# Three sums of squares a tile, from VectorE to ScalarE, in an expert retrieval that streams its rows by indirect DMA

## The reference

```
y   = gelu(y);  y = y * sigmoid(y @ w_glu + b_glu)        # 512 wide
mix = concat(rmsnorm(attn, g_attn), rmsnorm(y, g_ssm));   x = x + mix @ w_out
xn  = rmsnorm(x, g_ffn)
q   = xn @ w_query; s = q . sub_keys; per head (8): top 16 of each half,
      the 16 best of their sums -> idx, gate = softmax(best)     # 128 experts a token
out = x + sum_k gate_k * gelu(u_table[idx_k] . xn) * v_table[idx_k]
y   = rmsnorm(out, g_final)
rmsnorm(x, g) = x * (mean(x*x) + 1e-5) ** -0.5 * g
```

## Time and profile before

| | |
|---|---|
| median of three runs | 3325.18 us |
| profiled execution, its own time | 3328.39 us |
| its span, first to last instruction | 3326.6 us |
| PE matmul busy | 2289.7 us (69%) |
| VectorE (DVE) busy | 2177.2 us (65%) |
| GpSimd (POOL) busy | 1330.7 us (40%) |
| ScalarE (ACT) busy | 936.3 us (28%) |
| share of 16 DMA engines by the gathers' queue | 84.0% |
| bytes | 1216.94 MB, mean 366 GB/s |

### The profile page before, as it was taken

How to read it: one execution, slowest core, us unless ns; L and a number is a source line. 1 busy time by engine, 2 the same in 40 slices (tenths; PEclk the granted TensorE clock), 3 DMA queues, 4 the chain that set the end, 5 groups by cost and what they waited for, 6 DMA issues and landing times.

```text
span 3326.6 us, 31891 instructions
## 1 busy us (share of the span) xinstructions
PE 2289.7 (69%) x9269; PEld 938.1 (28%) x9269; DVE 2177.2 (65%) x5175; ACT 936.3 (28%) x3200; POOL 1330.7 (40%) x1272
## 2 busy tenths in 40 slices
PE   8997675766685668566855685568566855685576
PEld 4555451331151115111511151115111511151121
DVE  4544539788667756775677567756776676568654
ACT  2222114323332222222322232322232223222222
POOL 1241014434443444344434443444444444444442
PEclk9999787886896779687978797889688978797799
DMA  5223269999999999999999999999999999999998
GB/s 192 84 72 88 75 270 358 386 386 402 419 419 415 417 400 417 416 417 402 419 416 417 400 419 415 416 398 419 413 413 418 419 402 420 397 408 411 420 420 338
DMA packets 188351, 1216.94 MB, mean 366 GB/s; under 512 B 27272, under 2 KB 30712, under 8 KB 47456
## 3 DMA queue, kind: packets, MB, share of 16 engines
q0 software_dynamic: 157600, 1143.05, 84.0%
q1 hardware_dynamic: 30576, 71.86, 6.0%
HBM read 1199.15 MB, written 15.55 MB: 365 GB/s over the span
## 4 chain that ended last, share of the span: by engine, by line
DMA 33%; PE 22%; DVE 17%; issue 7%; ACT 5%; POOL 3%; another core or an unknown queue 0%; DVEq 0%; POOLq 0%; PEldq 0%; ACTq 0%; SPq 0%
DMA uv_ring<-in_uv_table,idx 33%; PE ACC L1998 14%; DVE uv_ring L1823 9%; PE TQ L1937 5%; POOL uv_ring L1465 3%; ACT dg L1598 2%; PE OP L1918 1%; ACT dot L1591 1%; PE TQ L1959 1%; ACT dot L1578 1%; DVE pos L1668 1%; DVE idx_f L1744 1%; DVE pos L1665 1%; DVE S L1743 1%; DVE best L1667 0%
## 5 line engine op out<-in xcount | busy, mean ns | idle before, releaser
L1998 PE MATMUL ACC<-uv_ring,dg 128*64 128x512 f32 x4352 | 1440.2, 772 | 932.5 <-ACT dg L1598 932.3
L1465 POOL DMA_INDIRECT uv_ring<-in_uv_table,idx x1088 | 1234.1, 1134 | 1611.2 <-PE ACC L1998 1375.1
L1823 DVE CUSTOM_DVE_ANT_0 uv_ring<-uv_ring,xn 128x1024 f32<-128x1024 f32 x1088 | 1326.5, 1226 | 738.2 <-DMA uv_ring<-in_uv_table,idx 675.5
L1998 PEld LDWEIGHTS ACC<-uv_ring,dg 128*64 128x64 f32 x4352 | 339.4, 164 | 1925.4 <-ACT dg L1598 1405.6
L1578 ACT ACTIVATE dot<-dot 128x2 f32<-128x2 f32 x544 | 110.5, 203 | 1853.6 <-DVE dot L1823 1838.8
L1598 ACT ACTIVATE dg<-stack,dot 128x64 f32<-128x64 f32 x1088 | 326.4, 340 | 17.8
L1591 ACT ACTIVATE dot<-gate,dot 128x1 f32<-128x1 f32 x1088 | 261.1, 287 | 18.9
L1937 PEld LDWEIGHTS TQ<-glu_and_queries,wq 128*128 128x128 f32 x2048 | 237.0, 194 | 63.9 <-issue 63.9
L1937 PE MATMUL TQ<-glu_and_queries,wq 128*128 128x128 f32 x2048 | 250.5, 281 | 0.0
L527 PE MATMUL PJ<-w_in,xT 128*128 128x512 f32 (+1 forms) x384 | 142.7, 528 | 3.2 <-DVE pj L407 3.2
L527 PEld LDWEIGHTS PJ<-w_in,xT 128*128 128x128 f32 x384 | 72.2, 191 | 68.1 <-issue 65.2
(11 more groups left out here) (336 smaller groups left out, 1640.2 us busy)
## 6 DMA issues: line engine op xcount, KB each, us to landing
uv_ring<-in_uv_table,idx POOLq DMA_INDIRECT x1088
glu_and_queries<-in_w_glu SPq DMA_DIRECT2D x9, 1024.0 KB
wq<-in_w_query SPq DMA_DIRECT2D x8, 1024.0 KB, 19.5
w_in<-in_w_in SPq DMA_DIRECT2D x8, 640.0 KB, 11.0
xt<-in_x SPq DMA_DIRECT2D x9, 512.0 KB, 4.7
xr<-scratch_x SPq DMA_DIRECT2D x9, 512.0 KB
xc<-in_x_columns SPq DMA_DIRECT2D x8, 512.0 KB, 3.8
xk<-in_x SPq DMA_DIRECT2D x8, 512.0 KB, 3.5
```

Of the source, the lines that this page charges most:

```text
L1465: pool.indirect_dma_start(out=ring[:, s_ % RING, :], out_offset=None, in_=a["uv_table"], in_offset=bass.IndirectOffsetOnAxis(ap=idx[:, s_: ...
L1823: V.tensor_tensor_reduce(row, row, xn[:, g, :], 1.0, 0.0, ALU.mult, ALU.add, dot[:, s_:s_ + 1]).then_inc(dots, 1)
L1998: ins = nc.tensor.matmul(ACC[GT * g:GT * (g + 1), b, :], dg[:, n % DG, :], ring[:, n % RING, D + 512 * b:D + 512 * b + 512], start=False, ...
```

## The change

The three sums of squares are taken by ScalarE as `Square` with `accum_out`, in the output tiles that VectorE used. The square of y stands at step (1, 4), that of x at (2, 7), that of the output at the end of ScalarE's turn, behind `begin(t + 1)` (the gelu, weights and diagonals of slots 0 and 1). VectorE's means move to (1, 6), (2, 9) and, as `mean_out`, to slot LEAD + 1 = 4 of the next tile; for the samples it follows `sum_out` directly. The later steps move on: POOL's roots to (1, 6) and (2, 9) and gather 12; VectorE's scaling of y to (1, 12) and of x to (2, 14); PE's turning of y from (1, 11) to (1, 14); VectorE's multiplication of turned y from (1, 13) to (1, 15); the scaling of the output from slot 6 to slot 8. `xr_done` is now marked by the second addition to x.

```diff
-        OUT_AT = LEAD + 3
+        OUT_AT = LEAD + 5
@@ POOL
-                        if turn != "first" and s_ == RING + LEAD:
+                        if turn != "first" and s_ == RING + LEAD + 1:
                             root("o", t - 1, ms_o, rs_o)
...
-                                if (h, j) == (1, 3):
+                                if (h, j) == (1, 6):
                                     root("y", t_, ms_y, rs_y)
-                                if (h, j) == (2, 6):
+                                if (h, j) == (2, 9):
                                     root("x", t_, ms_x, rs_x)
@@ ScalarE
+                    elif at == (1, 4):
+                        k["y_gated"].of(act, t)
+                        k["ss_y_done"].mark(A(z[:], y[:], ACT.Square, accum_out=ss_y))
+                    elif at == (2, 7):
+                        k["xr_done"].of(act, t)
+                        k["ss_x_done"].mark(A(xn_next[:], xr[:], ACT.Square, accum_out=ss_x))
...
                     if turn != "samples":
                         begin(t + 1)
+                    n = NS_ROWS if turn == "samples" else P
+                    k["acc_taken"].of(act, t)
+                    k["ss_o_done"].mark(A(squares[0:n, :], xo[0:n, :], ACT.Square, accum_out=ss_o[0:n]))
@@ VectorE
-                        dch_(V.tensor_tensor(y[:], y[:], z[:], ALU.mult))
-                        dch_(V.tensor_tensor_reduce(z[:], y[:], y[:], 1.0, 0.0, ALU.mult, ALU.add, ss_y))
+                        k["y_gated"].mark(V.tensor_tensor(y[:], y[:], z[:], ALU.mult))
+                    elif at == (1, 6):
+                        k["ss_y_done"].of(dve, t)
                         k["ms_y_done"].mark(V.tensor_scalar(ms_y, ss_y, 1.0 / SW, EPS, ALU.mult, ALU.add))
-                    elif at == (1, 9):
+                    elif at == (1, 12):
...
-                    elif at == (1, 13):
+                    elif at == (1, 15):
                         k["yn_turned"].of(dve, t)
...
-                        dch_(V.tensor_tensor(xr[:, 512:D], OP[:, 1, :], xr[:, 512:D], ALU.add))
-                        k["xr_done"].mark(V.tensor_tensor_reduce(xn_next[:], xr[:], xr[:], 1.0, 0.0, ALU.mult, ALU.add, ss_x))
-                        k["xr_done"].of(dve, t)
+                        k["xr_done"].mark(V.tensor_tensor(xr[:, 512:D], OP[:, 1, :], xr[:, 512:D], ALU.add))
+                    elif at == (2, 9):
+                        k["ss_x_done"].of(dve, t)
                         k["ms_x_done"].mark(V.tensor_scalar(ms_x, ss_x, 1.0 / D, EPS, ALU.mult, ALU.add))
-                    elif at == (2, 12):
+                    elif at == (2, 14):
...
-                    k["acc_taken"].of(dve, t)
-                    k["ss_o_done"].mark(V.tensor_tensor_reduce(squares[0:n, :], xo[0:n, :], xo[0:n, :], 1.0, 0.0,
-                                                               ALU.mult, ALU.add, ss_o[0:n]))
+
+                def mean_out(t, n):
+
                     k["ss_o_done"].of(dve, t)
                     k["ms_o_done"].mark(V.tensor_scalar(ms_o[0:n], ss_o[0:n], 1.0 / D, EPS, ALU.mult, ALU.add))
...
                         product(t, s_)
+                        if s_ == LEAD + 1 and turn != "first":
+                            mean_out(t - 1, P)
...
                         sum_out(t, NS_ROWS, t * NSLOT + slots_of(turn))
+                        mean_out(t, NS_ROWS)
                         norm_out(t, NS_ROWS)
@@ PE
-                    elif at == (1, 11):
+                    elif at == (1, 14):
                         k["yn_done"].of(pe, t)
```

More of the change, by code:

```diff
@@ L1367, in retrieve_experts @@
             "idx_ready idx_rest best_shifted ex_done gate_ready gate_rest xn_spread_a xn_spread_b xn_taken_a xn_taken_b acc_begun acc_taken "
-            "ss_o_done out_ready out_stored ms_y_done ms_x_done ms_o_done rs_y_done rs_x_done rs_o_done").split()}
+            "ss_o_done out_ready out_stored y_gated ss_y_done ss_x_done ms_y_done ms_x_done ms_o_done rs_y_done rs_x_done rs_o_done").split()}
         first = {n: c.sem(f"first_{n}") for n in "q qT s S topped nmax ex idx gate".split()}
@@ L1623, in begin @@
                         diagonal(t, s_)
-                for n in ("y_gelu yT_done gate_y xnT_done qT_a qT_b qT_c qT_d S_a S_b ex_done "
+                for n in ("ss_y_done ss_x_done ss_o_done y_gelu yT_done gate_y xnT_done qT_a qT_b qT_c qT_d S_a S_b ex_done "
                           "xn_taken_a xn_taken_b").split():
@@ L1862, in _ @@
                 for n in ("zb_done yn_done ynT_done xr_done xn_done topped_a topped_b idx_ready idx_rest best_shifted gate_ready gate_rest "
-                          "acc_taken ss_o_done out_ready ms_y_done ms_x_done ms_o_done").split():
+                          "acc_taken y_gated out_ready ms_y_done ms_x_done ms_o_done").split():
                     k[n].prime(dve)
```

## The result

Over 20 runs of each kernel on one chip the changed kernel takes 3330.5 us and the one before 3320.2 us, medians. The ratio is 1.0032, 95% interval 1.0021 to 1.0043: 10.5 us slower, 7 to 14. (Two of the changed kernel's 20 runs, 3538 and 7658 us, are slow ones and don't count in the ratio; without them its median is 3330.1 us.) The forecast was 3331.5 us against a median of 3325.2, so 6.3 us slower; that was the right side, at 0.6 of the size. The prediction took anything under 17 us as not to be told from no change; 20 runs of each tell 10.5 us from none. The profiled execution has a span of 3332.3 us.

A forecast was written before the change was run, and what follows sets the result against it. The prediction took the DMA engines to bound the kernel. Its terms, 0.4 (start and end) + 2.4 (tile 0) + 3.5 (x) + 0 (boundary) = 6.3 us, on 3325.2 gave 3331.5 us, spanning 3325 to 3343; 8-in-10 range 3310 to 3350.

The forecast's parts named there:

- What bounds the kernel: From tile 1 on the DMA engines set the pace; 128 gathers take 320 us of a tile's 331.
- The output norm at the boundary: At the tile boundary VectorE's wait for the root shrinks from 3.2 to about 1 us; gain 0, at best 3.5.
- The wait at slot 15: VectorE waits 5.5 us for turned y; the batch of 16 and 17 starts 3.0 us late, hidden by the lead.
- nothing covers it: Upper bound at gather 30 if no lead hides the delay: 3.0 us a tile, 21 us lost.
- the term of 0.5 us a tile: At gather 30, 1.7 us late, part is covered: 0.5 us lost in each of seven tiles, +3.5 us.
- Given on to x: The output projection comes 3 us late too, so VectorE's wait for it grows by up to 3 us a tile.
- Tile 0: VectorE is nearly always busy there; the turning makes it 4.5 us late, less the squares of y and x: +2.4 us.
- Before the first gather and at the end: Nothing covers ScalarE's squares there; handoffs cost 0.15 us for y, 0.1 for x, 0.15 for the last output: +0.4 us.
- the chain at its word: Rival: boundary work taken off VectorE shortens every tile, 3.4 x 7 = 24 us, giving 3301 us; chance 0.12.
- The table rival: Rival: Square needs another table than Gelu, so each square adds two loads: 3341 us, 3350 by the page; chance 0.05.
- That PE makes the delay up: Rival: PE catches up, 4 us gained at slot 30 and 3.5 at 1190, giving 3320 us; chance 0.05.
- The rival in which the wait starves the ring: Rival: slot 15's 3.0 us a tile aren't hidden, 21 us, plus 4.5 in tile 0, giving 3351 us; chance 0.20.

The follow-up runs named there:

- run 7: The kernel before with only the output's part of the change: its square on ScalarE, later mean, root and norm; 3326.7 us, ratio 0.9992.
- run 2: The kernel before, all squares on VectorE, with y turned at (1, 14) and multiplied at (1, 15); 3342.5 us, ratio 1.0078.
- run 8: The kernel before with only x's part of the change: its square on ScalarE, later mean, root and scaling; 3328.7 us, ratio 0.9994.
- Run 3: The changed kernel with VectorE's multiplication of turned y at (2, 0) instead of (1, 15), turning left at (1, 14); 3320.4 us, ratio 1.0003.
- Runs 1: The early turning: the changed kernel with PE turning y at (1, 12) instead of (1, 14); 3317.1 us, ratio 0.9995.
- Run 5: The changed kernel, late turning kept, with VectorE's addition to x, ScalarE's square and the mean two slots later; 3336.3 us, ratio 1.0024.
- run 9: The changed kernel with y turned at (1, 12) and the steps of x two slots later; 3321.1 us, ratio 0.9986.
- run 4: The changed kernel with y turned at (1, 12), except in tile 0's turn, which keeps (1, 14); 3316.5 us, ratio 0.9993.

## Why the prediction was right, and where its size was off

- **What bounds the kernel:** right. Every kernel here follows how full the DMA engines are: from the four with the least loss in the stretch (-0.1 to 2.2 us, ratios 0.9986 to 1.0002) to the three with the most (19.8 to 24.5 us, 1.0032 to 1.0078). VectorE's busy time does not order them: the changed kernel has 32 us less of it and is slower. The sign that I had named, a DMA share of 1.00 or more in tiles 1 to 7, held (1.00 or 1.01 in each); it is too coarse, for the rate fell in five of the seven tiles, in tile 2 from 413 to 408 GB/s.
- **The output norm at the boundary:** the wait fell as forecast (0.3 us in the mean), and the gap from gather 7 to gather 8 stayed: 6.0 us in tile 2 after, 6.3 before. The gain was taken as 0, at best 3.5. The two profiles have 3.9 us at the boundary and run 7 gives 2.7, with an interval that reaches no change. That the 3.9 us come from the output's part is not shown: in the same 28 us windows run 2, which has the old output norm, reaches 389.9 GB/s and run 8, which has it too, 386.3, as much as run 7's 386.3. So a gain of 0 isn't refuted.
- **The wait at slot 15:** right in place and size. 5.5 us were reckoned; tiles 1 to 7 have 5.1 to 6.2. So is what follows in tile 2, where the batch of 16 and 17 and gather 24 come 2.8 us late against the 3.0 reckoned. Over the seven tiles gather 24 is 2.8 to 6.3 us late, 4.2 in the mean.
- **The step that was mis-sized** is "*Gathers 24 and 25 are 3 us late. The lead hereabouts is far above 6.3 ...: hidden*", and with it the term of 0.5 us a tile, 3.5 in all. The profiles show 14.8 us, 2.1 a tile, which is nearer to the 3.0 of "nothing covers it" than to my 0.5. I read one lead, at slot 16, and took the next from slot 30. Between them it falls: in tile 2 before, the gathers of slots 24, 26 and 28 have 13.1, 9.1 and 8.4 us, the last two already within 3 us of the least. After, gather 26 was issued at 1226.65 and used at 1234.50, 7.9 us, and the engines had run dry around it. Gather 30, on which I put the whole loss, is over 2.4 us late in only three tiles of seven, and in tile 2 its lead rose from 6.3 to 9.1 us. I had written that I am wrong if a second hole opens around slots 24 to 32. The two short windows of tile 2 show such holes, so by that sign this step was wrong. Run 3 shows that the cover isn't nothing either: of 3.1 us of wait most is covered, of 5.7 it is not. Runs 1 and 2, and 5 against 9, show that this wait is the cause.
- **Given on to x:** the projection was late and VectorE's wait for it grew, by 28 us over tiles 1 to 7, 4.0 a tile, where I had said up to 3. I had read the 17.7 us before as a wait that these tiles have already; 8.9 of it stand ahead of the first gather. And it was not through this second wait that the loss came, as I had it (gather 30). Run 5 took it away and kept the loss.
- **Tile 0:** 2.4 us were reckoned, from a delay of 4.5. The wait is 3.4 us in the kernel after, and run 4 sees no cost of it, but can't tell 2.4 from 0.
- **Before the first gather and at the end:** too small to see. From the last copy to the end of the span there are 8.0 us before and 7.9 after.
- **The sum:** 0.4 + 2.4 + 3.5 + 0 = 6.3 us forecast. Measured by its own terms: 14.8 - 3.9 = 10.9 in the profiles, 10.5 by the ratio of all runs. That the forecast came to 0.6 of the measured time is luck in part: its main term was too small by 11 us, and the unconfirmed term of tile 0 and the gain at the boundary stood against that.
- **The rivals:** the chain at its word falls (run 7: 2.7 us instead of 8 or more). The table rival falls: no load was added. The Trainium skill, ScalarE: Activation LUTs, Table sets, says that cheap functions are filler in every set. It names relu, copy, identity and abs there and not Square, so I read it further than it goes; the trace agrees for Square, with 27 of them and 53 loads in all as before. (By its own numbers that rival's 2.7 us a tile are 2.8, and its 9 us more by the page 9.7; nothing hangs on it.) That PE makes the delay up falls too: in tile 2 it makes up less than 0.1 us of 2.8. The rival in which the wait starves the ring has the mechanism right and the cover wrong: its 21 us assume none, the profiles show 14.8. The measured case lies between it and my forecast, inside the forecast's own span.

What stays open: why the late turning costs 15 us more with the squares on VectorE (run 2) than with them on ScalarE, of which the profiles' losses show only 4; and what part of run 9's 4.7 us comes from where. The later steps of x alone are worth 0.08 to 0.09%, some 3 us, with the late turning and with the early one, and in neither case is that clear of the intervals.

## What to carry to other kernels

When steps of a hand-written order are moved on, keep their distances, and count them in rows behind the batch after which the producer's step really runs, not in slots. Here a producer moved by three slots and its consumer by two, and the two rows between them became none; that cost what three squares taken off VectorE could not pay back. Run 3 has the two slots of the kernel before again, 14 to 16 as 11 to 13, but only one row between, and still waits 3.1 us. Where a DMA ring sets the pace, a wait has an allowance that is mostly free, the queue ahead of the gather it delays; read that allowance at every slot in the delay's path, not at one, and count as cost only what exceeds it. A chain of waits that ends in a transfer six times longer than the transfer takes is a queue, and work saved in front of it was worth 2.7 us here, or nothing, where the chain promised 8 or more.

## What the runs showed that I had not expected

The cost is steep: a wait of 3.1 us a tile leaves the time within the noise of the kernel before (1.0003) and 3.3 us over the early turning, and one of 5.7 us costs 0.3 to 0.8%. And PE, which is busy 69% of the span and never looked like the limit, runs 15.5 us without a pause for the six slots of the projection, which is just the 2.5 us a row at which the DMA delivers; for that stretch it has no slack to give.
